# Normed tokens at another place in SBUF for each stage of a five-branch model, on one core

## The reference

```python
h = rms_norm(x, g)          # (256, 1024)
silu(h @ w1) * (h @ w3)     # an FFN: w1, w3 (1024, 2816), then @ w2 (2816, 1024)
z = h @ w_in                # a mixing stage: w_in (1024, 6752); in the second block a narrower one
```

## Time and profile before

| | us |
|---|---|
| median of three runs | 1715.36 |
| profiled execution | 1712.19 |
| its span | 1710.4 |
| TensorE matmuls busy | 1660.6 |
| TensorE weight loads busy | 1479.5 |
| VectorE busy | 1060.1 |
| ScalarE busy | 814.2 |
| GpSimd busy | 232.0 |

### The profile page before, as it was taken

How to read it: one execution, slowest core, us unless ns; L and a number is a source line. 1 busy time by engine, 2 the same in 40 slices (tenths; PEclk the granted TensorE clock), 3 DMA queues, 4 the chain that set the end, 5 groups by cost and what they waited for, 6 DMA issues and landing times.

```text
span 1710.4 us, 27114 instructions
## 1 busy us (share of the span) xinstructions
PE 1660.6 (97%) x11162; PEld 1479.5 (87%) x11162; DVE 1060.1 (62%) x1255; ACT 814.2 (48%) x1109; POOL 232.0 (14%) x204
## 2 busy tenths in 40 slices
PE   7999999999999999999999999999999998999898
PEld 7999888889989998999978897989999877787785
DVE  4555657665764556555567755775555597756875
ACT  5443546643454435443355653444434553645453
POOL 0000240010000000000051010000000078003930
PEclk9999999999999999999999999999999989998999
DMA  7657454433546554656645342455555452254511
GB/s 237 223 179 231 149 181 148 144 120 103 182 145 214 180 187 149 219 180 206 201 158 179 110 148 75 152 193 194 179 192 185 138 189 75 81 160 161 167 57 62
DMA packets 207892, 275.02 MB, mean 161 GB/s; under 512 B 19030, under 2 KB 168376, under 8 KB 207288
## 3 DMA queue, kind: packets, MB, share of 16 engines
q1 hardware_dynamic: 206376, 272.67, 48.8%
q10 hardware_dynamic: 1424, 1.05, 0.2%
HBM read 271.61 MB, written 1.08 MB: 159 GB/s over the span
## 4 chain that ended last, share of the span: by engine, by line
PE 84%; DVE 9%; ACT 3%; issue 2%; POOL 1%; ACTq 1%; DMA 0%; SPq 0%; POOLq 0%; DVEq 0%
PE bank L503 28%; PE bank L550 13%; PE bank L986 8%; PE bank L975 7%; PE bank L2034 5%; PE bank L1171 4%; DVE wlo L435 3%; PE bank L1253 2%; PE bank L2283 2%; ACT whi L424 2%; PE bank L2012 2%; PE bank L2129 1%; PE bank L1089 1%; DVE hT_lo L354 1%; PE bank L1050 1%
## 5 line engine op out<-in xcount | busy, mean ns | idle before, releaser
L435 DVE TENSOR_TENSOR wlo<-raw,whi 128x2048 fp32r<-128x2048 f32 (+1 forms) x258 | 583.1, 2263 | 334.0 <-ACT whi L424 333.6
L424 ACT ACTIVATE whi<-raw 128x2048 fp32r<-128x2048 f32 (+1 forms) x258 | 484.0, 1880 | 347.2 <-PE bank L550 101.4
L503 PE MATMUL bank<-hT_hi,whi 128*128 128x256 f32 x1408 | 395.7, 281 | 0.9 <-DVE hT_lo L354 0.5
L503 PE MATMUL bank<-hT_lo,whi 128*128 128x256 f32 x1408 | 394.1, 280 | 0.0
L503 PE MATMUL bank<-hT_hi,wlo 128*128 128x256 f32 x1408 | 393.9, 280 | 0.0
L503 PEld LDWEIGHTS bank<-hT_hi,whi 128*128 128x128 f32 x1408 | 266.3, 189 | 4.1 <-issue 1.8
L503 PEld LDWEIGHTS bank<-hT_lo,whi 128*128 128x128 f32 x1408 | 266.4, 189 | 1.4
L503 PEld LDWEIGHTS bank<-hT_hi,wlo 128*128 128x128 f32 x1408 | 266.3, 189 | 0.0
L550 PE MATMUL bank<-whi,Y 128*128 128x512 f32 x704 | 224.0, 390 | 0.0
L550 PEld LDWEIGHTS bank<-whi,Y 128*128 128x128 f32 x704 | 132.2, 188 | 26.7
L308 POOL TENSOR_TENSOR st<-st 128x1 f32<-128x1 f32 x18 | 18.6, 1039 | 955.8 <-ACT X L301 955.8
(11 more groups left out here) (393 smaller groups left out, 2864.7 us busy)
## 6 DMA issues: line engine op xcount, KB each, us to landing
raw<-in_ffn_w SPq DMA_DIRECT2D x132, 1024.0 KB, 5.3
raw<-in_w_in SPq DMA_DIRECT2D x80, 1024.0 KB, 5.4
raw<-in_w_out SPq DMA_DIRECT2D x16, 1024.0 KB, 4.9
raw<-in_w_br_na SPq DMA_DIRECT2D x4, 1024.0 KB, 5.0
raw<-in_w_br_mla SPq DMA_DIRECT2D x4, 1024.0 KB, 5.1
raw<-in_w_br_gla SPq DMA_DIRECT2D x4, 1024.0 KB, 5.8
raw<-in_cmp_k_w SPq DMA_DIRECT2D x4, 1024.0 KB, 7.4
raw<-in_cmp_v_w SPq DMA_DIRECT2D x4, 1024.0 KB, 5.2
```

Of the source, the lines that this page charges most:

```text
L424: act.activation(m["whi"][:, slot, 0:w], m["raw"][:, slot, 0:w], ACT.Copy).then_inc(s.hi_ready, 1)
L435: dve.tensor_tensor(m["wlo"][:, slot, 0:w], m["raw"][:, slot, 0:w], m["whi"][:, slot, 0:w].bitcast(F32), ALU.subtract).then_inc(s.lo_ready, 1)
L503: mm = pe.matmul(B[bank][:, mt * T:(mt + 1) * T], a, b, start=(n == 0 and k == 0), stop=(n == KK - 1 and k == 2))
```

## The change

High and low part become one tile, `tokens`, of 2 x 8 x 256 + 32 floats, allocated before x. `hT(norm)` gives the two parts at a place that depends on the stage: TOKEN_PLACE holds, in floats, 4, 12, 12, 24, 16, 16, 2, 20 for n = 0 to 7, that is 16, 48, 48, 96, 64, 64, 8 and 80 bytes. The low part follows 8192 bytes behind the high part, so both lie at that place modulo 1024. The tiles behind move with it: `tokens` takes 16512 bytes, so x begins at 128 modulo 1024 where it was 0, and KEEP, consts and those behind them lie 128 bytes further modulo 1024. All instructions, their order and their waits stay.

```diff
+TOKEN_PLACE = (4, 12, 12, 24, 16, 16, 2, 20)
...
+        tokens = sb("tokens", [P, 2 * KK * T + 32], F32R)
         x = sb("x", [P, NT, D + 1])
-        hT_hi = sb("hT_hi", [P, KK, T], F32R)
-        hT_lo = sb("hT_lo", [P, KK, T], F32R)
...
-        hT = lambda kk, a=0, n=T: (hT_hi[:, kk, a:a + n], hT_lo[:, kk, a:a + n])
+
+        def hT(norm):
+
+            at = TOKEN_PLACE[norm]
+            return [tokens[:, a:a + KK * T].rearrange("p (k t) -> p k t", k=KK) for a in (at, at + KK * T)]
...
-        act.activation(m["hT_hi"][:, kk, t * P:(t + 1) * P], self.xT(banks, kk, t), ACT.Copy,
+        act.activation(m["hT"](n)[0][:, kk, t * P:(t + 1) * P], self.xT(banks, kk, t), ACT.Copy,
...
-        dve.scalar_tensor_tensor(m["hT_lo"][:, kk, t * P:(t + 1) * P], self.xT(banks, kk, t),
-                                 gain[:, kk:kk + 1], m["hT_hi"][:, kk, t * P:(t + 1) * P].bitcast(F32), ALU.mult,
+        high, low = m["hT"](n)
+        dve.scalar_tensor_tensor(low[:, kk, t * P:(t + 1) * P], self.xT(banks, kk, t),
+                                 gain[:, kk:kk + 1], high[:, kk, t * P:(t + 1) * P].bitcast(F32), ALU.mult,
...
-                    for k, (a, b) in enumerate(passes(w, self.m["hT"](kk))):
+                    for k, (a, b) in enumerate(passes(w, [part[:, kk, :] for part in self.m["hT"](self.norm)])):
...
+    hT = lambda kk, a=0, n=T: [part[:, kk, a:a + n] for part in m["hT"](n0 + 1)]
```

More of the change, by code:

```diff
@@ L363, in act_high_both @@
             act.wait_ge(s.hT_ready, 2 * K_ORDER.index(kk - 1) + 2)
-        act.activation(m["hT_hi"][:, kk, :], m["B"][banks[kk // 2]][:, (kk % 2) * T:(kk % 2 + 1) * T], ACT.Copy,
+        act.activation(m["hT"](0)[0][:, kk, :], m["B"][banks[kk // 2]][:, (kk % 2) * T:(kk % 2 + 1) * T], ACT.Copy,
                        scale=gain[:, kk:kk + 1]).then_inc(s.hThi_ready, 2)
@@ L369, in dve_low_both @@
         dve.wait_ge(s.hThi_ready, 2 * i + 2)
-        dve.scalar_tensor_tensor(m["hT_lo"][:, kk, :], m["B"][banks[kk // 2]][:, (kk % 2) * T:(kk % 2 + 1) * T],
-                                 gain[:, kk:kk + 1], m["hT_hi"][:, kk, :].bitcast(F32), ALU.mult,
+        high, low = m["hT"](0)
+        dve.scalar_tensor_tensor(low[:, kk, :], m["B"][banks[kk // 2]][:, (kk % 2) * T:(kk % 2 + 1) * T],
+                                 gain[:, kk:kk + 1], high[:, kk, :].bitcast(F32), ALU.mult,
                                  ALU.subtract).then_inc(s.hT_ready, 2)
@@ L791, in first_layer @@
     unit = lambda step: UM + MIX_FIRST[step]
-    par, st, X, G, Y, KEEP, B, C, x, hT = (m[k] for k in ("par", "st", "X", "G", "Y", "KEEP", "B", "C", "x", "hT"))
+    par, st, X, G, Y, KEEP, B, C, x = (m[k] for k in ("par", "st", "X", "G", "Y", "KEEP", "B", "C", "x"))
+    hT = lambda kk, a=0, n=T: [part[:, kk, a:a + n] for part in m["hT"](n0 + 1)]
     gain = [par[:, 8 * n:8 * n + 8] for n in range(3)]
@@ L1896, in second_layer @@
     XT = (3, 4, 5, 6) if l else (2, 3, 4, 5)
-    par, st, X, G, Y, KEEP, B, C, x, hT = (m[k] for k in ("par", "st", "X", "G", "Y", "KEEP", "B", "C", "x", "hT"))
+    par, st, X, G, Y, KEEP, B, C, x = (m[k] for k in ("par", "st", "X", "G", "Y", "KEEP", "B", "C", "x"))
+    hT = lambda kk, a=0, n=T: [part[:, kk, a:a + n] for part in m["hT"](n0)]
     ident_r, mask_r = m["ident_r"], m["mask_r"]
```

## The result

The change makes the kernel slower: 1722.83 us median (1720.37 to 1725.79, five runs) against 1713.92 us (1711.94 to 1716.21, five runs), a ratio of 1.005 with a 95% interval of 1.0035 to 1.0065, +8.9 us. The profiled execution took 1725.18 us, 13.0 more than the one of before.

A forecast was written before the change was run, and what follows sets the result against it. TensorE, busy 1660.6 of 1710.4 us, was taken as the bound. Moving tokens +13.5 and stationary -3.3 gave +10.2 us on 1712.19, so 1722.4; with the median 3.2 above that execution, 1725.5, range 1697 to 1746.

The forecast's parts named there:

- 48 bytes: Mixing stage and second FFN of layer 0: nearest row is that of 32, so no change, 1728 matmuls, 0.
- 64 bytes: Mixing stage and second FFN of layer 1: 120.0 ns, +3.3 ns for each of 1728 matmuls, +5.7 us.
- Does the place matter at all?: Only addresses differ; 3.5 ns between same-shape groups read as stationary load and moving read holding each other up by their stagger.
- 16 bytes: First FFN: halfway between 0 and 32, 118.3 ns, +1.7 ns for each of 1056 matmuls, +1.8 us.
- The middle of three excesses: Tokens moving at 64, 96, 80 bytes: middle of 10.0, 13.5, 20.0 ns, rounded to 120.0 ns per matmul, +3.3 ns.
- Tokens stationary: Mixing stages and second layers, 512 columns moving: 0 at 48 bytes, -2.3 at 64, -0.6 at 80, -0.4 at 8; -3.3 us.
- 8 bytes: First second layer, tokens moving: three quarters of the way to 0, 119.2 ns, +2.5 ns x 432, +1.1 us.
- The other tiles' shift: x, KEEP and constants move 128 bytes; some 500 matmuls by 3.5 ns either way are 1.8 us, taken as 0.
- The floor: Lower bound for tokens moving at new places: 114.2 ns, from matmuls beside a load of only 32 columns.
- The much slower one: Leads of 64 or 96 act like -32 if the pattern repeats every 96 to 128 bytes: +29 us, 1744; chance 17%.
- The faster one: Excess keeps falling with lead, so 48, 64, 80, 96 reach 114.2 ns: -18 us, 1697, halfway 1706; chance 27%.
- The rule of lines of 16 bytes: Each crossing to a new SBUF line costs; at 8 bytes off, 65 lines instead of 64, 0.7 us by estimate.

## Why the prediction held, and where its steps did not

The direction and the size were right: 1725.5 forecast, 1722.83 measured; +10.2 forecast, +8.9 between the medians (the forecast began at a median of 1715.36 from three runs, five gave 1713.92). That the place sets the pace was right too; how it does so is only shown in part. The closeness of the sum is luck between terms: for the four FFNs +8.8 was booked and +8.7 measured, but 48 bytes was booked 2.0 too low there and 64 bytes 2.3 too high, and elsewhere +4.7 for moving and -3.3 for stationary tokens were booked, of which the chain shows little more than the term for 80 bytes (17.28 against 16.82 us for 144).

- **"Does the place matter at all?"** Yes: 3.5 ns between two groups of the same shape were the sign of it, and tokens at 0 now have the pace that Y at 0 had, 119.9 ns against 120.2. With the old place in the new layout the effect is gone, and it goes with the place from stage to stage. The Trainium skill's rule in "TensorE: Matmul & The Clock Gate", "Step-by-step: what each phase is for", that the load takes no read bandwidth from the running matmul, would make the pace independent of what the load reads, and these traces do not agree with that: a load that sweeps nothing gives back 3.0 to 4.3 ns of each matmul at four of five places. Whether it is bandwidth that the load takes, or something else, no run shows.
- **Readings of the rows.** Two of the 40 slices of the granted clock show an 8 and not "nine tenths or more", both late in the span, where the second layers have 0.95 and 0.96; in the FFNs it is 1.00. "32 bytes behind" and "32 bytes ahead" mean the same place, tokens 32 bytes past a multiple of 1024. That the average over weights at 0 and at 512 is 116.7 did not yet show a repetition within 512 bytes; the single matmuls do: in the pair of the earlier trace rows the first 24 (weights at 0) start at 59.93 us, the next 24 (at 512) at 62.73 and those after them at 65.53, 116.7 ns each both times.
- **16 bytes**, between 0 and 32: 118.3 ns forecast, 118.6 measured (11.39 / 96), +1.8 us both. **96**: 120.0 forecast and measured, +3.5 against +3.7 us. **80**: 120.0 both (17.28 / 144), but the same place had 118.4 in the other layer (17.05 / 144). The middle of three excesses was a good guess for 96 and 80 and no more than that.
- **48 bytes**, "nearest row is that of 32, no change": failed. It is 118.4 ns, +2.0 us in the FFN. Nearness in bytes says nothing, as 108, 112 and 116 show.
- **64 bytes**, 120.0: too high. 117.8 ns, and for 168 tall matmuls of the mixing stage 19.79 us as before; +1.2 us in the FFN where +5.7 was booked for it and the mixing stage.
- **Tokens stationary**, -3.3 us, of which 2.3 at 64 bytes: failed. 233.3 ns stays at 48 and 64 bytes, as at 32. The places that do gain, 256 (226.8) and 120 (226.7), were not in the change.
- **8 bytes**, +2.5 ns: failed as far as the chain shows it. 144 tall matmuls take 16.81 us as before, in either layer of the second block; the rest of that layer is mixed with the clock.
- **The other tiles' shift**, taken at 0: right.
- **The floor.** The 114.2 ns of the narrow load was used as a bound that whole loads would hardly reach. The whole load reaches 113.8 at a lead of 112.
- **Rivals.** The much slower one rested on a repetition every 96 to 128 bytes; 112 against 16 and 144 against 16 rule that out, and no FFN took more than 121.7 ns. The faster one named about the right floor by the wrong reason: there is no trend with the lead, but one place, 112, at which the load costs next to nothing in every FFN. The rule of lines of 16 bytes ("SBUF — State Buffer", "Specifications (TRN2)", of the Trainium skill) fits the neighbours of 112, for all of 104, 108, 116 and 120 are slow and cross one line more, but not the size: 0.7 us was worked out for 432 matmuls, 1.7 ns each, and 4 bytes off cost 6 to 8. It also fails at 8 bytes, where a row crosses one line more as well: 16.81 us for 144, like 32 bytes and 0.5 us less than the 17.29 of 0.

What stays open: why the lead decides when the weights are read 64 or 32 bytes earlier or 32 later, and when both operands move by 32, but not when the weights are read 80 bytes earlier (a run with both operands moved by 16 was not made); why 112 escapes the load; what is left at 0 and 96 bytes when the load sweeps nothing; and what picks the pace where one place has two: 113.3 or 117.8 ns at 64 bytes, 118.4 or 120.0 at 80, 116.8 or 117.8 at 32.

## What to carry to other kernels

Where TensorE is the bound, divide the time of a run of equal matmuls in the chain by their count and compare groups of one shape: a difference of 3 ns between them can come from addresses alone, and here such a difference is worth 1% of the kernel. An address is then to be measured place by place and not interpolated; several stages of one kernel can each carry a place, and one profile reads them all. Change one operand's lead over the other; moving all tiles together by 32 bytes did nothing here. And look at every stage: what is a fast place for moving tokens (112) is a slow one for stationary tokens, and at 32, 64 and 80 bytes one place had two paces.

## What the runs showed of the hardware

- The pace of a 256-column fp32r matmul by the moving operand's lead over its stationary block in SBUF, whole load, us per 96 in a steady FFN: 0 bytes 11.51, 16 11.39, 32 11.20, 48 11.37, 64 11.31, 80 11.51, 96 11.52, 104 11.61, 108 11.51, 112 10.92, 116 11.68, 120 11.58, 144 11.20, 160 11.40, 176 11.44, 192 11.31, 208 11.44, 256 11.51. The value at 80 is from the layout moved by 32 bytes. In the second block, us per 144: 8 bytes 16.81, 128 17.09, and two values at one place, 16.34 and 16.97 at 64, 17.05 and 17.28 at 80; tokens at 32, too, had 16.82 before and 16.97 in the run with the weights read at another place.
- Part of the excess goes with the sweep of the load. The matmul beside a load that sweeps nothing takes 113.4 to 113.6 ns at 32, 64 and 112 bytes and 116.7 at 0 and 96, over 106.7 for its columns; the sweep of the load adds 0.3 to 4.3 ns.
- A narrower load does not help in proportion: 64 columns 116.9 ns, 32 columns 117.5, against 120.0 with 128.
- Reversed, with 512 columns of weights moving, the matmul takes 233.3 ns with stationary tokens at 32, 48, 64 and 112 bytes, 234.2 at 96, 226.8 at 256 and 226.7 at 120.
